# A gated-DeltaNet stage on one core: inverses of 16x16 blocks on GpSimd, and a regrouped chunk

## The chip, the cores and the metric

The kernel runs on one core of a Trainium2 chip. The metric is device time of one execution in microseconds (us). Three runs of the kernel before gave 1876.74 us (median), 1874.43 and 1877.13. Everything is float32.

## The reference

Two layers over 512 latent tokens and 256 context tokens, 1024 channels. Each layer has an input projection, latent attention (4 heads), a bidirectional gated DeltaNet (4 heads of 128), a pooling branch, an output projection and a mixture of experts. The change is in the DeltaNet alone. The reference computes it in chunks, for every chunk and head:

```python
decay = exp(where(incl, gc[:, None] - gc[None, :], -inf))
a_low = where(strict, (kb @ k.T) * decay, 0.0)       # kb = k * beta
tmat  = a_low + eye(C)
w = solve(tmat, kb * exp(gc)); u = solve(tmat, v * beta)   # unit lower triangular
qk = (q @ k.T) * decay
# then, chunk after chunk, with the state s
v_new = u - w @ s
o     = (q * exp(gc)) @ s + qk @ v_new
s     = s * exp(g_last) + (k * exp(g_last - gc)).T @ v_new
```

The backward direction runs the same on reversed tokens, over context and then latent tokens too.

## The kernel before

The 768 tokens are six tiles (chunks) of 128 tokens, j = 0 to 5; in chunk j both directions d = 0, 1 work, each on its own tile, with four heads h. Everything of the stage is kept transposed: state `minus_S`, keys, queries, decays `gE` and `gQG`.

For every chunk the kernel builds X, the inverse of the unit triangular 128x128 matrix, by doubling. Each half of 64 rows is treated apart, for both directions and four heads at a time. The identity minus the entries inside blocks of 2 is the inverse at level 0. At level n = 1 to 5 (blocks of 2, 4, 8, 16, 32) GpSimd (POOL) cuts the entries that join two blocks out of the matrix (`masked`, semaphore `ml`), TensorE (PE) multiplies them by the transposed inverse (`level_factor`, L955), VectorE (DVE) writes identity minus that into `gW` (L2391), PE multiplies once more for both X and its transpose (`level_update`, L973), and ScalarE (ACT) copies the four products back to `gXC` (L1887). Each step of a level waits for the one before. A last step joins the two halves: `z6` (L1058), ACT's two negated copies (L1892), `u6` (L1070), DVE's copies into `gX`. POOL copies the diagonal halves into `gX` (L2830, semaphore `xd`), and `v` of the chunk, the product X by the right side, needs all of it.

The rest of the chunk's work is put between the levels, by a table `BETWEEN`: 13 slots per chunk, slot 2n-1 between the two products of level n and slot 2n behind them. Its entries are `v` (L889), `go` (output, L900 and L901), `st` (state update, L906), `kr` (keys turned, L871), `kk` (key-key products of the next chunk, L863), `ks` (values turned, minus keys by state, L879 and L882), `qk` (query-key products of the next chunk, L866) and `g` (decays of the next chunk). In layer 0 one half of a modulation load (`ada_load`, L571, eight matmuls and 1 MB of weights per pair of halves) stands in each of slots 0 to 11. Each engine walks the same slots in its own program order. Banks of PSUM go round in a ring of eight.

Ahead of the stage stands the attention, 24 calls (tile, head) in layer 0 and 16 in layer 1; the first chunk's `g`, `kk` and level 0 are set among its last eight calls (`first_chunk`). ACT's exponentials of call n are L1855. POOL does next to nothing there.

In the first chunk ACT also has eight SiLU passes (L1727, L1874) and two loads of its function table.

## Time and profile before

| | us |
|---|---|
| median of three runs | 1876.74 |
| lowest and highest | 1874.43, 1877.13 |
| profiled execution, whole | 1878.56 |
| its span, first to last instruction | 1876.4 |
| PE busy | 1765.4 (94%) |
| DVE, ACT, POOL busy | 716.7, 471.4, 433.8 |

The profile is of one execution. Busy time of PE counts modelled ends of pipelined matmuls. A matmul of float32 stands in the profile as two instructions, so 16 matmuls of the program are x32. The recurrent stage, the subject here, lies from 365.9 to about 590 us (layer 0) and from 1337.9 to about 1520 us (layer 1). A chunk is counted from the end of one `u6` (L1070) to the end of the next.

### The profile page before, as it was taken

Reading aid. Unit: us, or ns where it says so; the run is one execution under the profiler, and the core shown is the slowest. Engines: PE = TensorE matmul, PEld = TensorE weight load, DVE = VectorE, ACT = ScalarE, POOL = GpSimd, SP = SyncE. Lnnn points to the kernel's source line nnn. Section 1 sums busy time; section 2 is a strip of 40 time slices with the busy share of each in tenths; the row PEclk is TensorE's granted clock in tenths of the full one; section 3 lists DMA queues with packets and bytes.
Section 4 is the critical chain, followed back from the end, with each engine's and each line's share of the span. In section 5 each row is a group of like instructions: output and inputs, shape, how many; then the busy total and the mean of one; then the engine's idle time right before and its main releaser. Section 6 shows DMA issues by size and latency. Waiting matters only on the chain.

```text
span 1876.4 us, 40908 instructions
## 1 busy us (share of the span) xinstructions
PE 1765.4 (94%) x17273; PEld 1087.7 (58%) x17273; DVE 716.7 (38%) x1452; ACT 471.4 (25%) x1051; POOL 433.8 (23%) x556
## 2 busy tenths in 40 slices
PE   6999999989999998999999999999888899899998
PEld 4565556667776554655566455556577854445544
DVE  3045233455554234111211506334466633432323
ACT  4211422443234041111110321333433222101010
POOL 2713000255651003111110142200277710000000
PEclk9999999999999998999999999999999999999999
DMA  9510000265555217999998421000300022599996
GB/s 311 169 60 23 23 0 1 96 202 188 181 174 206 67 45 272 344 372 371 366 328 326 122 67 45 23 1 2 103 26 14 15 113 90 222 408 413 408 413 240
DMA packets 140855, 321.24 MB, mean 171 GB/s; under 512 B 11208, under 2 KB 98894, under 8 KB 125358
## 3 DMA queue, kind: packets, MB, share of 16 engines
q1 hardware_dynamic: 127584, 287.20, 41.2%
q0 software_dynamic: 6432, 20.00, 4.1%
q10 hardware_dynamic: 6702, 12.05, 2.0%
q8 instruction: 107, 1.75, 0.4%
q14 instruction: 30, 0.25, 0.0%
HBM read 305.77 MB, written 13.45 MB: 170 GB/s over the span
## 4 chain that ended last, share of the span: by engine, by line
PE 84%; DVE 7%; issue 3%; ACT 2%; DMA 2%; SPq 1%; POOL 0%; ACTq 0%; DVEq 0%; POOLq 0%
PE psum L654 16%; PE psum L1204 12%; PE psum L1104 7%; PE psum L1235 6%; PE psum L786 3%; PE psum L1213 3%; PE psum L1285 3%; PE psum L973 3%; PE psum L807 2%; PE psum L571 2%; PE psum L955 2%; PE psum L679 2%; PE psum L1247 2%; PE psum L889 1%; PE psum L839 1%
## 5 line engine op out<-in xcount | busy, mean ns | idle before, releaser
L654 PE MATMUL psum<-hT,ring 128*128 128x512 f32 (+3 forms) x880 | 298.9, 497 | 0.0
L654 PEld LDWEIGHTS psum<-hT,ring 128*128 128x128 f32 (+1 forms) x880 | 165.7, 190 | 121.3 <-issue 111.0
L1204 PE MATMUL psum<-ring,arena 128*64 128x256 f32 x1536 | 176.3, 387 | 6.0 <-DVE xT L2553 3.6
L1204 PEld LDWEIGHTS psum<-ring,arena 128*64 128x64 f32 x1536 | 110.1, 139 | 69.4 <-issue 14.9
L1104 PE MATMUL psum<-hT,ring 128*128 128x512 f32 (+1 forms) x384 | 139.4, 521 | 0.9 <-DVE xT L2437 0.9
L2524 DVE TENSOR_TENSOR arena<-arena,psum 128x384 f32<-128x384 f32 (+1 forms) x32 | 15.6, 488 | 260.8 <-PE psum L1213 159.8
L1104 PEld LDWEIGHTS psum<-hT,ring 128*128 128x128 f32 x384 | 72.7, 190 | 64.8 <-issue 61.5
L973 PE MATMUL psum<-wbuf,ring 64*64 64x64 f32 x1920 | 76.1, 225 | 30.6 <-DVE wbuf L2391 18.9
L1887 ACT COPY ring<-psum 128x256 f32<-128x256 f32 x240 | 72.8, 382 | 127.6 <-PE psum L973 127.6
L2870 POOL DMA_INDIRECT big<-h_rows_lat,idx x16 | 15.7, 979 | 377.9 <-PE psum L1309 175.4
L2391 DVE TENSOR_TENSOR wbuf<-lev,psum 128x256 f32<-128x256 f32 x120 | 45.1, 417 | 137.0 <-PE psum L955 137.0
L973 PEld LDWEIGHTS psum<-wbuf,ring 64*64 64x64 f32 x1920 | 66.6, 137 | 49.2 <-issue 47.7
L2553 DVE SCALAR_TENSOR_TENSOR xT<-psum,modraw,xT 128x512 f32<-128x512 f32 (+1 forms) x136 | 79.7, 621 | 18.8 <-PE psum L1285 12.8
L786 PE MATMUL psum<-hT,ring 128*128 128x256 f32 (+1 forms) x192 | 80.8, 530 | 0.0
L1965 ACT COPY arena<-psum 128x512 f32<-128x512 f32 (+2 forms) x49 | 23.6, 481 | 221.2 <-PE psum L1226 147.1
L2176 DVE SCALAR_TENSOR_TENSOR big<-psum,cols,big 128x511 f32<-128x511 f32 (+1 forms) x44 | 27.6, 628 | 126.9 <-ACT big L1720 125.9
L973 PE MATMUL psum<-ring,wbuf 64*64 64x64 f32 x1920 | 73.5, 225 | 1.2 <-issue 1.2
L1285 PE MATMUL psum<-arena 128*128 128x512 f32 x144 | 65.8, 602 | 4.4 <-DVE arena L2540 2.7
L1969 ACT ACTIVATE arena<-psum 128x384 f32<-128x384 f32 (+1 forms) x32 | 14.0, 438 | 212.5 <-PE psum L1204 107.6
L973 PEld LDWEIGHTS psum<-ring,wbuf 64*64 64x64 f32 x1920 | 63.0, 137 | 1.6 <-issue 1.5
L571 PE MATMUL psum<-ring,scol 128*32 128x256 f32 x768 | 60.2, 399 | 3.5 <-issue 2.6
L2223 DVE TENSOR_REDUCE small<-psum 128x1 f32<-128x768 f32 (+1 forms) x40 | 33.9, 851 | 77.2 <-PE psum L807 75.3
(358 smaller groups left out, 3327.8 us busy)
## 6 DMA issues: line engine op xcount, KB each, us to landing
ring<-in_moe_w_gate SPq DMA_DIRECT2D x64, 1024.0 KB, 10.5
ring<-in_ada_w SPq DMA_DIRECT2D x48, 1024.0 KB, 5.4
ring<-in_moe_w_up SPq DMA_DIRECT2D x32, 1024.0 KB, 9.7
hT<-in_moe_w_down SPq DMA_DIRECT2D x24, 1024.0 KB
ring<-in_w_in SPq DMA_DIRECT2D x20, 1024.0 KB, 7.3
big<-in_moe_w_up SPq DMA_DIRECT2D x16, 1024.0 KB, 10.8
sz<-in_moe_w_down SPq DMA_DIRECT2D x16, 1024.0 KB
big<-in_moe_w_down SPq DMA_DIRECT2D x16, 1024.0 KB
```

Source lines behind the costliest of these rows:

```text
L571: m = pe.matmul(ada[1][r:r + 32, 0:SLOT_COLS], lhsT=scol[:, 2 * k:2 * k + 32], rhs=ada[2][:, k, :], start=half == 0, stop=half == 1)
L654: m = pe.matmul(b[0:c1 - c0, 0:n], lhsT=w[:, k, c0:c1], rhs=hT[:, k, t0:t0 + n], start=k == 0, stop=k == KD - 1)
L786: x = pe.matmul(b[:, 0:n], lhsT=w[:, k, m % 2 * P:(m % 2 + 1) * P], rhs=hT[:, k, t0:t0 + n], start=k == 0, stop=k == KD - 1)
L973: m = pe.matmul(bs[kind][o, i * HALF:(i + 1) * HALF], lhsT=v if transposed else w, rhs=w if transposed else v, start=True, stop=True)
L1104: m = pe.matmul(b[:, 0:x], lhsT=w[:, k, c:c + P], rhs=mixT[:, k, t0:t0 + x], start=k == OUT_REST[0], stop=k == OUT_GDN[-1])
L1204: m = pe.matmul(b[e * CAP_L:(e + 1) * CAP_L, 0:2 * P], lhsT=xs[:, k, e, 0:CAP_L], rhs=w[e][:, 2 * (k - ks[0]) + q, :], start=k == 0, stop= ...
L1213: m = pe.matmul(b[r:r + CAP_C, 2 * P:3 * P], lhsT=xs[:, k, e, CAP_L:CAP], rhs=v[:, 2 * (k % (KD // 2)) + q, f * P:(f + 1) * P], start=k == ...
L1235: m = pe.matmul(ys[c][e * CAP_L:(e + 1) * CAP_L, :], lhsT=hidT[:, q, f * P + e * CAP_L:f * P + (e + 1) * CAP_L], rhs=w[e][:, f, c * 512:(c ...
L1285: m = pe.matmul(b[:, 0:SEQ], lhsT=ylat[:, k * P:(k + 1) * P], rhs=Sl[:, :], start=True, stop=True)
L1887: read_out(act.copy(gXC[j % 2][:, d, w:w + GH, :].rearrange("p h c -> p (h c)"), b), key)
L2391: read_out(dve.tensor_tensor(gW[:, :, h0:h0 + 2, :], eyes, b, ALU.subtract), key)
L2553: read_out(dve.scalar_tensor_tensor(out=x, in0=b[:, 0:n], scalar=mods_of[l][:, 5 * KD + k, 1 - g:2 - g], in1=x, op0=ALU.mult, op1=ALU.add) ...
```

## The change

Levels 1 to 3 are gone. The inverses of all 16x16 diagonal blocks, of both directions, six tiles and four heads, are made once per layer during the attention: 3072 bytes per partition, one block per 256 numbers, three blocks in each of the 128 partitions ("lanes").

- In attention call 1 PE makes the key-key products of 32 tokens each (`pk`, 96 matmuls of 128x32 by 32 columns, four beside each other in the output partitions); DVE keeps the 16x16 diagonal blocks. In call 2 ACT writes them to device memory (`kkD`, pieces of 64 bytes), POOL reads them back as lanes, together with decay sums and beta.
- POOL takes differences, ACT the two functions of them (call 7), POOL multiplies, and then solves by 15 steps of an outer product and a subtraction, each waiting for the one before. POOL writes the inverses out (`xD`), ACT reads them back per chunk (`blocks_back`), POOL spreads them over the block diagonal (`spread`), and PE turns them (`diagonal_blocks`) as it did with level 0.
- ACT waits in the third last attention call for the inverses to be written.
- A chunk now has levels 4 and 5 and 7 slots. `qk` of a chunk stands at that chunk's end instead of the end of the one before, `kk` and the turned blocks of the next chunk beside it, both `ks` in one slot, both `v` in one slot. In layer 0 both halves of a modulation load stand in each of slots 0 to 5.
- The decays of the next chunk are no longer subtracted on DVE: ACT takes the four heads with a bias each. They stand in slots 3 and 5.
- On POOL the one-sided decays and the masks follow the copies of the diagonal halves.

```diff
 BETWEEN = (
-    (("v", 0),), (("v", 1),), (("go", 0),), (("go", 1),), (("st", 0), ("st", 1)),
-    (("g", 0),), (("g", 1), ("kr", 0)), (("kr", 1),), (("kk", 0),), (("kk", 1),), (("ks", 0),), (("qk", 0),),
-    (("ks", 1), ("qk", 1)))
-G_SLOTS = (6, 8)
+    (("v", 0), ("v", 1)), (("go", 0),), (("go", 1),), (("st", 0), ("st", 1)),
+    (("kr", 0), ("kr", 1), ("kk", 0)), (("ks", 0), ("ks", 1)), (("kk", 1), ("t0", 0), ("qk", 0), ("qk", 1)))
+G_SLOTS = (3, 5)
+LANES_EXP = 7
...
+                    if n == 1:
+                        pe.wait_ge(s["lmul"], GH)
+                        for w in range(2):
+                            b = claim(("pk", l, w))
+                            for x in range(NT * GH // 2):
+                                i, h = divmod(w * NT * GH // 2 + x, GH)
+                                for q in range(4):
+                                    t = slice(i * P + 32 * q, i * P + 32 * (q + 1))
+                                    m = pe.matmul(b[32 * q:32 * (q + 1), 32 * x:32 * (x + 1)], lhsT=qkvT[:, GH + h, t],
+                                                  rhs=qkvT[:, GH + h, t], start=True, stop=True)
...
-                    for n in range(1, LEVELS - 1):
-                        pe.wait_ge(s["ml"], (LEVELS - 1) * j + n + 1)
+                    for n in range(FROM, LEVELS - 1):
+                        pe.wait_ge(s["ml"], 2 * j + n - FROM + 1)
                         level_factor(j, n, x)
-                        gdn_between(j, 2 * n - 1)
-                        if n == 1:
-                            pe.wait_ge(s["x0"], j + 1)
+                        gdn_between(j, 2 * (n - FROM) + 1)
                         for d in range(2):
                             level_update(j, n, x, d)
-                        gdn_between(j, 2 * n)
+                        gdn_between(j, 2 * (n - FROM) + 2)
...
+                def next_decays(j, d):
...
+                    for h in range(GH):
+                        m = act.activation(e[:, h, :], q[:, h, :], ACT.Abs, bias=gc[:, d, i, h:h + 1], scale=-1.0)
+                    m.then_inc(s["away"], 1)
...
+                    act.activation(e, e, ACT.Exp, scale=-1.0).then_inc(s["away"], 1)
+                    act.activation(q, q, ACT.Exp).then_inc(s["away"], 1)
...
+                    act.copy(gt4[:, j % 2, d, 0, :], e[:, :, end])
+                    act.copy(gt4[:, j % 2, d, 1, :], q[:, :, end]).then_inc(s["dex"], 1)
...
+                    if slot in G_SLOTS and 1 <= j < NT - 1:
+                        next_decays(j + 1, G_SLOTS.index(slot))
+                    if slot == 4 and j + 2 < NT:
+                        act.wait_ge(s["x0"], j + 2)
+                        blocks_back(j + 2)
...
+                    if n == 2:
+                        for w in range(2):
+                            evacuated(act, ("pk", l, w))
+                        act.dma_start(kkD[l].rearrange("x p c -> p x c"), pairs16).then_inc(s["pairs"], 16)
...
+                    if n == 5:
+                        act.wait_ge(s["xout"], 32 * (l + 1))
+                        blocks_back(0)
+                        blocks_back(1)
...
+                pool.tensor_tensor(lane_y, across(lane_g), down_(lane_g), ALU.subtract).then_inc(s["ldiff"], 1)
+                pool.wait_ge(s["lexp"], 2 * (l + 1))
+                link(pool.tensor_tensor(lane_a, lane_a, lane_y, ALU.mult), l)
...
+                for k in range(BLOCK - 1):
+                    n, w = BLOCK - 1 - k, k + 1
+                    t = lane_t[:, 0:3 * n * w].rearrange("p (s r c) -> p s r c", s=3, r=n)
+                    link(pool.tensor_tensor(t, lane_a[:, :, w:BLOCK, k:w].to_broadcast([P, 3, n, w]),
+                                            lane_y[:, :, k:w, 0:w].to_broadcast([P, 3, n, w]), ALU.mult), l)
+                    x = lane_y[:, :, w:BLOCK, 0:w]
+                    link(pool.tensor_tensor(x, x, t, ALU.subtract), l)
...
+                    if j >= 2:
+                        decay_state(j - 1, 0)
+                    if j + 1 < NT:
+                        spread(j + 1)
+                    if j >= 2:
+                        decay_state(j - 1, 1)
                     if j:
+                        decayed_keys(j, 0)
+                        decayed_keys(j, 1)
                         queries(j)
                     if j + 1 < NT:
                         decays(j + 1)
...
                     pool.wait_ge(s["xd"], j + 1)
                     if j + 1 < NT:
-                        begin(j + 1)
+                        one_sided(j + 1)
+                        masks(j + 1)
```

Two places show how instructions moved. The first is PE in layer 1, from the end of a full chunk into the next one. Before: L879 and L882 are `ks` of direction 1, L866 `qk`, L933 the turned blocks, L889 `v`, L955 and L973 the two products of level 1.

```order
L879 MATMUL psum<-ident,big 128x128
L882 MATMUL psum<-arena 128x128
L866 MATMUL psum<-big 128x128 x4
L933 MATMUL psum<-lev,mlaw 64x64 x16
L889 MATMUL psum<-arena,ring 128x128 x4
L955 MATMUL psum<-ring,mlaw 64x64 x16
L889 MATMUL psum<-arena,ring 128x128 x4
L973 MATMUL psum<-wbuf,ring 64x64 x2
```

Now: L1104 is `u6`, L885 `kk`, L958 the turned blocks, L888 `qk`, L911 `v`, L980 the first product of level 4, L922 and L923 `go`.

```order
L1104 MATMUL psum<-wbuf,ring 64x64 x8
L885 MATMUL psum<-big 128x128 x4
L958 MATMUL psum<-lev,ring 64x64 x16
L888 MATMUL psum<-big 128x128 x8
L911 MATMUL psum<-arena,ring 128x128 x8
L980 MATMUL psum<-ring,mlaw 64x64 x16
L922 MATMUL psum<-arena 128x128
L923 MATMUL psum<-arena 128x128
```

`ks` has moved ahead of `u6`; `kk`, the turned blocks and both `qk` stand between `u6` and `v`; and from the first factor PE goes to `go` and level 4.

The second place is ACT in layer 1, within a full chunk. Before: L1887 are the copies of X, L1795 to L1802 the decays of the next chunk (directions 0 and 1), L1892 the copies of `z6`.

```order
L1887 COPY ring<-psum 128x256 x8
L1795 ACTIVATE arena<-arena 128x512
L1797 ACTIVATE small<-small 128x8
L1800 ACTIVATE arena<-arena 128x512
L1802 ACTIVATE arena<-arena 128x512
L1887 COPY ring<-psum 128x256 x4
L1795 ACTIVATE arena<-arena 128x512
L1797 ACTIVATE small<-small 128x8
L1800 ACTIVATE arena<-arena 128x512
L1802 ACTIVATE arena<-arena 128x512
L1887 COPY ring<-psum 128x256 x4
L1892 ACTIVATE wbuf<-psum 128x128 x2
```

Now: L1964 are the copies of X, L1841 to L1849 the decays of direction 0 and, last row, the first of direction 1, L1854 the blocks of the chunk after next, L1969 the copies of `z6`.

```order
L1964 COPY ring<-psum 128x256 x4
L1865 DMA arena<-decay_rows 128x512
L1841 ACTIVATE arena<-arena,small 128x128 x4
L1845 ACTIVATE arena<-arena 128x512
L1846 ACTIVATE arena<-arena 128x512
L1848 COPY small<-arena 128x4
L1849 COPY small<-arena 128x4
L1964 COPY ring<-psum 128x256 x4
L1854 DMA blocks_in<-inverse_blocks 128x4x16 x2
L1969 ACTIVATE wbuf<-psum 128x128 x2
L1841 ACTIVATE arena<-arena,small 128x128 x4
```

The decays of direction 0 stand ahead of the last level's copies, those of direction 1 behind the copies of `z6`.

## Rows read from the trace of the kernel before

**Rows 1.** windows: length, busy us and (xcount) by engine, granted clock, DMA share, GB/s

```profile
365.90:590.00 224.10, 203.74 (x4522) 155.38 (x4523) 116.00 (x245) 81.41 (x224) 122.45 (x147) 0.98 0.61 194
1337.90:1520.00 182.10, 152.47 (x3861) 135.16 (x3860) 108.56 (x235) 65.49 (x187) 114.82 (x141) 0.96 0.08 25
472.30:510.40 38.10, 34.56 (x769) 26.71 (x770) 21.48 (x44) 12.39 (x36) 23.24 (x28) 1.00 0.57 183
1421.30:1452.50 31.20, 26.96 (x675) 24.28 (x674) 20.87 (x45) 9.76 (x30) 22.91 (x27) 1.00 0.07 20
365.90:399.50 33.60, 27.48 (x661) 18.87 (x661) 15.58 (x35) 20.21 (x46) 14.89 (x20) 0.95 0.74 237
1337.90:1364.00 26.10, 17.30 (x537) 14.78 (x538) 13.34 (x32) 17.39 (x40) 9.48 (x15) 0.86 0.23 74
```

**Rows 2.** timeline of PE, layer 0: start us, us, engine, line, out<-in, count

```profile
403.22 0.69 PE L955 MATMUL psum<-ring,mlaw 64*64 64x64 f32 x32
403.85 1.16 PE L889 MATMUL psum<-arena,ring 128*128 128x128 f32 x8
...
405.51 0.27 PE L973 MATMUL psum<-wbuf,ring 64*64 64x64 f32 x2
...
406.60 0.60 PE L901 MATMUL psum<-arena 128*128 128x128 f32 x3
```

**Rows 3.** waits of PE in the recurrent stage of layer 1

```profile
PE psum L973 <- DVE wbuf L2391: 16.1, 17, 1.5
```

**Rows 4.** timeline of PE, a full chunk of layer 1

```profile
1428.14 0.49 PE L900 MATMUL psum<-arena 128*128 128x128 f32 x2
...
1430.12 0.69 PE L955 MATMUL psum<-ring,mlaw 64*64 64x64 f32 x32
```

**Rows 5.** timeline of ACT, the same chunk

```profile
1441.16 0.63 ACT L1795 ACTIVATE arena<-arena 128x512 f32<-128x512 f32 x1 [1.75 <-DVE small L2268]
...
1442.84 1.17 ACT L1887 COPY ring<-psum 128x256 f32<-128x256 f32 x4
...
1450.42 0.45 ACT L1892 ACTIVATE wbuf<-psum 128x128 f32<-128x128 f32 x2 [2.02 <-PE psum L1058]
```

**Rows 6.** timeline of POOL, the same chunk

```profile
1445.75 1.04 POOL L2710 TENSOR_TENSOR arena<-arena,small 128x512 f32<-128x512 f32 x1 [1.70 <-ACT arena L1802]
1446.75 2.50 POOL L2721 TENSOR_TENSOR arena<-arena,tri 128x512 f32<-128x512 f32 x2
1449.40 0.39 POOL L2830 COPY ring<-ring 64x256 f32<-64x256 f32 x1 [0.16 <-POOL arena L2721]
...
1451.24 0.72 POOL L2731 TENSOR_TENSOR mlaw<-dT,lev 128x256 f32<-128x256 f32 x1
```

**Rows 7.** timeline of DVE, the same chunk

```profile
1437.20 1.28 DVE L2318 TENSOR_TENSOR arena<-arena,psum 128x512 f32<-128x512 f32 x2
```

**Rows 8.** DMA issues: KB each, median us to landing

```profile
arena<-decay_rows ACTq DMA_DIRECT2D x20, 256.0 KB, 4.0
```

**Rows 9.** timeline of ACT, first chunk of layer 1

```profile
1337.86 1.28 ACT L1727 ACT_TABLE_LOAD   x1
1339.16 0.85 ACT L1727 ACTIVATE big<-big 128x768 f32<-128x768 f32 x1
```

**Rows 10.** timeline of PE in the attention, products into 64 output partitions

```profile
1307.04 0.27 PE L839 MATMUL psum<-wbuf,arena 128*64 128x128 f32 x1
...
1307.15 0.27 PE L839 MATMUL psum<-wbuf,arena 128*64 128x128 f32 x1
```

**Rows 11.** timeline of ACT in the attention of layer 1

```profile
1284.86 0.91 ACT L1855 ACTIVATE ring<-psum,small 128x768 f32<-128x768 f32 x1
...
1317.11 0.91 ACT L1855 ACTIVATE ring<-psum,small 128x768 f32<-128x768 f32 x1
```

**Rows 12.** timeline of POOL in the attention of layer 1

```profile
1303.45 1.04 POOL L2710 TENSOR_TENSOR ring<-ring,small 128x512 f32<-128x512 f32 x1 [108.67 <-ACT ring L1802]
```

**Rows 13.** DMA queues (packets, MB, share of 16 engines)

```profile
q10 hardware_dynamic: 6702, 12.05, 2.0%
```

More of the change, by code:

```diff
@@ L49 @@
 LEVELS = 7
+BLOCK = 16
+FROM = 4
 HALF = P // 2
@@ L305, in build_program @@
         gc = small[:, 96:144].rearrange("p (d i h) -> p d i h", d=2, i=NT)
+        beta = small[:, 144:192].rearrange("p (d i h) -> p d i h", d=2, i=NT)
+        gc_beta = small[:, 96:192]
+        lane_g = small[:, 192:240].rearrange("p (s r) -> p s r", s=3)
+        lane_b = small[:, 240:288].rearrange("p (s r) -> p s r", s=3)
         krp = small[:, 436:628].rearrange("p (i c) -> p i c", i=NT)
@@ L948, in level_factor @@
                         for i, pair in enumerate(((0, 3), (1, 2))):
-                            if i and n > 1:
+                            if i and n > FROM:
                                 evacuated(pe, ("x", l, j, d, n - 1))
@@ L1804, in decay_rows, with blocks_back @@
+                def blocks_back(j):
+                    for d in range(2):
+                        act.dma_start(blocks_in[:, j % 2, d * GH:(d + 1) * GH, :],
+                                      xD[l][d, tile_of(d, j)].rearrange("h p c -> p h c")).then_inc(s["xin"], 16)
                 def decay_rows(j, d):
@@ L1880, in _ @@
                     gdn_between(j, 0)
-                    for n in range(1, LEVELS - 1):
-                        gdn_between(j, 2 * n - 1)
+                    for n in range(FROM, LEVELS - 1):
+                        gdn_between(j, 2 * (n - FROM) + 1)
                         for d in range(2):
@@ L2384, in _ @@
                 for j in range(NT):
-                    if j:
-                        inverse_of_blocks(j)
-                    for n in range(1, LEVELS - 1):
+                    for n in range(FROM, LEVELS - 1):
+                        gdn_between(j, 2 * (n - FROM))
                         for h0, name in ((0, "zo"), (2, "zd")):
@@ L2693, in _ @@
                     m.then_inc(s["row2"], 1)
-                pool.wait_ge(s["gbd"], 1)
-                pool.wait_ge(s["lmul"], GH)
-                product_ready(pool, ("gc", l))
+                pool.wait_ge(s["pairs"], 16 * (l + 1))
+                for d in range(2):
+                    pool.dma_start(lane_a[d * HALF:(d + 1) * HALF].rearrange("p s r c -> p (s r c)"),
+                                   kkD[l].rearrange("x p c -> (x p c)").rearrange("(m e) -> m e", e=LANE)
+                                   ).then_inc(s["lanes"], 16)
@@ new lines, in _, with across, down_ @@
+                pool.wait_ge(s["grow"], 16)
+                pool.dma_start(small[:, 192:288].rearrange("p (w x) -> p w x", w=2),
+                               gD[l].rearrange("w d i h c -> w (d i h c)").rearrange("w (m x) -> m w x", x=3 * BLOCK)
+                               ).then_inc(s["lanes"], 16)
+                pool.wait_ge(s["lanes"], 48 * (l + 1))
+                def across(rows_, n=P):
+                    return rows_.unsqueeze(3).to_broadcast([n, 3, BLOCK, BLOCK])
+                def down_(rows_, n=P):
+                    return rows_.unsqueeze(2).to_broadcast([n, 3, BLOCK, BLOCK])
@@ L2727, in masked @@
                     a = gA if j else gA0
-                    first = a[:, :, 0:2, :] if n == 0 else a[:, :, GH:GH + 2, :]
-                    second = a[:, :, 2:8:5, :] if n == 0 or n % 2 else a[:, :, 2:4, :]
-                    mask = lev[:, :, n, :].unsqueeze(2).to_broadcast([P, 2, 2, HALF])
+                    first = a[:, :, GH:GH + 2, :]
+                    second = a[:, :, 2:8:5, :] if n % 2 else a[:, :, 2:4, :]
+                    mask = lev[:, :, n - FROM, :].unsqueeze(2).to_broadcast([P, 2, 2, HALF])
@@ L2791, in _ @@
                 decays(0)
-                begin(0)
-                third_mask(0)
+                masks(0)
+                how = freed_by[lent_prior[l]]
+                product_ready(pool, how[0], how[1])
+                spread(0)
                 pool.wait_ge(s["att"], 1)
                 one_sided(0)
-                pool.wait_ge(s["ml"], 3)
+                pool.wait_ge(s["ml"], 2)
                 if l == 0:
```

309 lines of the change are left out of this document (166 added, 143 removed).

## The prediction

> **What bounds the kernel now.** I read the windows first. The recurrent stage is 224.1 us in layer 0 and 182.1 us in layer 1, 406.2 of a span of 1876.4, and PE is busy for 203.74 and 152.47 of it; the reader is to see that no other engine reaches 70% there [rows 1]. A full chunk of layer 0 takes 38.1 us with 34.56 of PE, one of layer 1 31.2 with 26.96 [rows 1]. So layer 0 is bound by how much PE has to do, and layer 1, without modulation loads, by PE and some waiting. The table of waits says for what: in layer 1 second products of a level (L973) wait 17 times, 16.1 us in all, for DVE's copy between the two products [rows 3]. Then the timelines of one chunk give the price of a step on each engine [rows 2, 4 to 7]. The attention ahead keeps PE nearly full, while POOL stands idle for 108.67 us in layer 1 before its first decay [rows 12]: that is where the new work goes.
>
> **What goes.** A level packed without a wait is one factor, 403.22 to 403.85, 0.63 us, and two updates, 405.51 to 406.60, 1.09 us: 1.72 us of PE [rows 2]. Three of five go in each of six chunks and two layers: 36 x 1.72 = 62 us of PE, 31 per layer. With them go 36 x 4 copies on ACT and as many handoffs, whose waits are the rest of the gain or its loss, depending on what stands in their place. Four of the six masks of a chunk go from POOL, and the subtraction of decays from DVE; neither bounds anything.
>
> **The chunk that is left, layer 1.** PE's own work is 26.96 - 3 x 1.72 = 21.8 us [rows 1, 2]. Against it stands a loop through the other engines, since the decays have moved next to the copies. From the first state product of a chunk: `st` on PE 1.1 (eight instructions as L889, 403.85 [rows 2]), its addition on DVE 0.64 [rows 7], ACT's decays of direction 0, the last copies of X 1.2, `z6` 0.4 (half the instructions of a factor), its two copies 0.45, the decays of direction 1, POOL's beta product 1.04, four copies of 0.45 (0.39 and the handoff) 1.8, two one-sided decays 2.5, the first mask, two instructions of 0.72, 1.4, the factor 0.63, `go` 1.98, the update 1.09, `go` 1.98, the factor 0.63 [rows 2, 4 to 7]. ACT's decays of one direction are four passes over 128, two over 512 and two tiny ones. A pass over 128 is 0.22 (two in 0.45), one over 512 0.63, at a pitch of some 0.53 [rows 5]: 0.9 + 1.1 + 0.2 and two handoffs of 0.15, 2.5. The sum is 21.8 with the decays twice; 15 handoffs of 0.15 (0.16 is what POOL's wait for itself shows [rows 6]) make it 24.1. So the loop, not PE, sets a full chunk of layer 1: 24 us for 31.2, a gain of 7. With neither handoffs nor queues behind each other it would be 22, with 0.3 a handoff and the two issues of `blocks_back` in line 27. I take 24, because the masks and decays stand back to back on POOL already. `go` and its `qk` are missing in chunks 1 and 2 of this layer, so their loop is some 4 us shorter, and PE idles about 4.6 us in each.
>
> **Layer 0.** PE's own work of a full chunk is 34.56 - 5.2 = 29.4 [rows 1]. The loop is 24 plus two slots of loads inside it, which cost PE half of 34.56 - 26.96 = 7.6 at most: under 28. So PE bounds it still, and I add 1 us for what does not fit: 30.4 for 38.1. The loads have the same bytes in less time: 183 GB/s become 230, and the first chunk moves 237 already [rows 1], so the queue hides them.
>
> **First chunk.** Here ACT becomes the bound. It has the table load 1.3, eight SiLU passes of 0.85 and less [rows 9], a second table load, and, new, both directions' decays of chunk 1 ahead of the last copies, 5 us. In layer 1 that is 1.3 + 5.5 + 1.3 + 5 + 8 copies of 0.3 = 15.5 from 1337.86, so `z6` comes at about 1353.5 and `u6` ends near 1355: 17 us instead of 26.1. Layer 0 adds the loads' copies and issues, about 7: 24.5 instead of 33.6. PE is idle for some 9 us in each.
>
> **Sum of the stage.** By PE's busy time: layer 0 203.7 - 31 = 172.7, idle 9 in the first chunk, 1 in each other and 1.5 in the tail, 188, so 36 less. Layer 1: 152.5 - 31 = 121.5, idle 9, twice 4.6, twice 2.3, and 2 at the end, 146, so 36 less. By chunks instead (9 + 7 + 3 x 7.7 + 3.5, less 2.2 for the `qk` that moved behind the last `u6`) layer 0 gives 40, layer 1 about 42. The two counts differ by tails of matmuls that the busy time holds and a chain does not. I take 74 for both layers, nearer to the busy count, which has fewer of my own steps in it.
>
> **What the attention gets.** (a) PE: 96 products are 192 instructions per layer. Into 64 output partitions and 128 columns one takes 54 ns (two in 0.107 us at L839 [rows 10]), into quarters of 64x64 20 ns (32 in 0.63 [rows 2]). So 3.8 to 10.4 us; the new ones have 32 columns and four stand beside each other, nearer to the second: 5. (b) DVE and ACT in the same calls: two masks from PSUM, two additions, the decay sums two calls after the gates instead of many; PE waits 1.5 for the chain gate, sum, copy. Together 6.5 per layer, 13, with 8 and 26 as ends. (c) The lanes on POOL. An instruction of n elements costs 0.19 + 0.0021 n us (128x256 0.72, 128x512 1.25 [rows 6]) and 0.16 for its wait. Fifteen steps handle 3 x 680 elements twice, 4080: 8.5 + 30 x 0.35 = 19. Three products of 768 are 5.8, clearing and turning 2.8: 27.6 us. In layer 1 ACT makes the two functions in call 7, at 1284.86, 1.8 us long, and wants the inverses in call 13, at 1317.11 [rows 11]: 32.3 - 1.8 = 30.5 us, less a landing of 4.0 or under [rows 8]. That is a draw; what ACT waits there holds up the copies and exponentials of the last three calls. Ends: 0, and with POOL twice as slow 27. I take 2. In layer 0 there are 14 calls between, so nothing. (d) The pieces of 64 bytes, 3072 of them to write: a packet of ACT's queue takes 0.02 x 16 x 1876 / 6702 = 90 ns on one of 16 engines [rows 13], at 1.8 KB each, so 17 us at most and likely under half. It fits between calls 2 and 7.
>
> A rule that speaks against (c): POOL's instructions here cost 2.1 ns an element [rows 6]. The Trainium skill, GPSIMD Engine Reference, section 7, says that a read whose step is over 8 bytes costs half as much again for each element. No row here has such a step. If all of the solver's products paid it, they would take 4 us longer by that page, which makes the wait in layer 1 likelier and changes no term of mine.
>
> (e) The clock. In the stage's first chunk, where PE waits most, the granted clock reads 0.86 in layer 1 and 0.95 in layer 0, and 1.00 in full chunks [rows 1]. That is 26.1 x 0.14 = 3.7 us lost; PE will be idle there for 9 us at a stretch, so I add 3 for both layers, with 0 and 10 as ends.
>
> **Total.** -74 + 13 + 2 + 3 = -56. The profiled execution took 1878.56, 1.8 above the median of the runs, so 1822.5 of its kind and 1821 for the median.
>
> **Rivals.** *More is hidden* (6%): handoffs cost 0.05 and the chain count of the stage holds, -82 + 8: 1803. For it speaks that PE's gaps in full chunks are small now; against it the loop. *The lanes come late in layer 1* (15%): rows too short for POOL's pace, a solver of 45 us instead of 27.6; ACT stands in call 13 for 17 us with three calls' exponentials and copies behind it, POOL's masks and DVE's `kk` behind those: 1838. *The loop bounds both layers* (13%): 28 us in layer 1 and 33.5 in layer 0, as ACT's queue of loads' issues, decays, `blocks_back` and copies is one line: 7 x 4 more, 1850. For it speaks that PE's wait in L973 is already 16.1 us [rows 3]. *Slower* (5%): the same solver, at 70 us or above. The slack is 30 us in layer 1 and, 14 calls for 6, about 70 in layer 0; so layer 1 loses T - 28 and layer 0 T - 70, which eats the 56 at T = 77, 2.8 times my sum; 1881 at 80. Against it: 680 elements a lane is little, and even a fixed 1 us for each of 30 instructions makes only 45 in all. *It does not do what it says* (1%): the levels are gone from PE's order, so hardly.
>
> **Chances.** My forecast 60%, its own range 1808 to 1834. Faster 0.93, within 0.2% (what a measurement here can tell, 3.8 us) 0.02, slower 0.05. The range goes from 1802, past the terms' favourable ends, to 1854, past the loop rival.
>
> **What would show it.** Chunks of 30 and 24 us; first chunks of 24.5 and 17 with an idle stretch of PE under ACT's decays; 36 x 48 products fewer; the solver's 30 instructions in under 30 us, ending before the third last call of layer 1; attention 6 to 9 us longer. I am wrong if full chunks of layer 1 stay above 27, if ACT stands waiting for the written inverses, or if POOL has instructions of over 1 us for under 200 elements.

## The result, and the profile after

The changed kernel took 1801.4 us (median of 4 runs, 1800.3 to 1807.1) beside 1876.9 for the kernel before on the same chip: a ratio of 0.960, 95% interval 0.958 to 0.963. The forecast was 1821 with a range of 1802 to 1854. It is faster by 75 us, not by 56, and the time lies 0.6 us below the lower end of that range (the same kernel run again, 1805.5, lies inside it).

The profiled execution spans 1798.7 us. Its windows (length, busy time and instruction count of PE, PEld, DVE, ACT and POOL, granted clock, DMA share, GB/s) stand in the order of [rows 1]: the stage of each layer, a full chunk of each, the first chunk of each.

```profile
380.70:556.00 175.30, 162.89 (x2800) 130.05 (x2799) 85.95 (x183) 69.24 (x193) 89.36 (x106) 0.95 0.80 251
1308.10:1446.00 137.90, 115.62 (x2134) 105.80 (x2134) 79.10 (x171) 54.22 (x156) 81.50 (x100) 0.94 0.13 34
464.15:491.70 27.55, 26.76 (x481) 21.84 (x481) 14.75 (x32) 10.31 (x33) 17.71 (x21) 1.00 0.80 256
1391.80:1414.80 23.00, 20.77 (x385) 19.34 (x386) 14.58 (x34) 8.06 (x26) 17.31 (x21) 1.00 0.09 25
380.70:410.20 29.50, 20.41 (x347) 13.83 (x345) 7.36 (x17) 18.63 (x42) 10.68 (x14) 0.71 0.87 277
1308.10:1327.20 19.10, 11.17 (x250) 9.87 (x249) 6.89 (x15) 15.61 (x36) 5.67 (x10) 0.76 0.37 118
```

The reader is to see that a full chunk of layer 0 fell from 38.1 to 27.6 us with PE as full as ever, and one of layer 1 from 31.2 to 23.0 with 2.2 us of PE's time idle. The first chunks gained less, and their clock is 0.71 and 0.76, where it was 0.95 and 0.86.

To compare kernels I cut each layer in two: the attention, from its first exponential to the end of ACT's last copy, and the stage, from there to the end of the last update of the last chunk. All lengths below are cut so; us:

| kernel | attention L0 | L1 | stage L0 | L1 | median | ratio to before |
|---|---|---|---|---|---|---|
| before | 111.4 | 81.0 | 214.3 | 173.7 | 1876.9 | 1 |
| after | 127.9 | 86.2 | 164.0 | 127.7 | 1801.4 | 0.960 [0.958, 0.963] |
| after, run again | 127.7 | 87.8 | 164.0 | 128.2 | 1805.5 | 0.961 [0.957, 0.964] |
| levels out alone | 111.5 | 81.5 | 173.1 | 137.0 | 1800.1 | 0.957 [0.956, 0.959] |
| solver twice | 128.4 | 100.1 | 164.1 | 128.2 | 1819.3 | 0.968 [0.966, 0.970] |
| spread first | 125.9 | 83.7 | 163.4 | 128.6 | 1797.6 | 0.956 [0.955, 0.958] |
| masks first | 128.3 | 86.2 | 162.8 | 122.8 | 1800.3 | 0.958 [0.957, 0.960] |
| loads in separate groups | 128.9 | 86.1 | 169.0 | 128.2 | 1809.3 | 0.963 [0.961, 0.965] |
| `ks` in separate slots | 124.9 | 86.1 | 162.6 | 127.1 | 1803.5 | 0.960 [0.958, 0.962] |
| `pk` in separate calls | 124.9 | 86.0 | 164.9 | 128.5 | 1803.4 | 0.960 [0.957, 0.963] |
| `pk` twice | 132.8 | 93.4 | 165.3 | 128.3 | 1819.2 | 0.968 [0.966, 0.971] |
| combined | 121.1 | 84.5 | 162.8 | 122.6 | 1788.4 | 0.951 [0.948, 0.953] |

The same kernel moved by 4 us from one comparison to another, and layer 0's attention by 3 where nothing in it was changed (`ks` in separate slots). So differences of medians below 4 us are read from the stretches, not from the totals. Where that 3 comes from can be seen in the attention of layer 0 as a whole, first after, then `ks` in separate slots, then `pk` in separate calls:

```profile
252.77:380.68 127.91, 111.92 (x857) 73.94 (x857) 48.86 (x114) 34.93 (x86) 31.62 (x50) 0.96 0.07 17
252.65:377.58 124.93, 109.04 (x857) 72.01 (x857) 48.85 (x114) 34.96 (x86) 31.62 (x50) 0.99 0.07 18
254.36:379.27 124.91, 112.03 (x857) 74.06 (x857) 48.68 (x114) 34.96 (x86) 31.62 (x50) 0.96 0.08 18
```

The first two kernels give PE the same 857 instructions in the same order. It is busy 2.9 us longer at a granted clock of 0.96 than at 0.99, and the stretch is 3.0 us longer. So the clock moves this stretch by 3 us between executions of the same code. The third is as short at the lower clock.

The stage gave back 50.2 + 46.0 = 96.2 us and the attention took 16.6 + 5.2 = 21.7 (worked out before rounding). That leaves 74.5 of the 77.7 between the spans.

What binds a full chunk of layer 0 now, PE in the trace of after (start us, us, engine, line, out<-in, count):

```profile
464.08 1.16 PE L885 MATMUL psum<-big 128*128 128x128 f32 x8
465.17 0.69 PE L958 MATMUL psum<-lev,ring 64*64 64x64 f32 x32
465.79 2.05 PE L888 MATMUL psum<-big 128*128 128x128 f32 x16
467.68 1.95 PE L911 MATMUL psum<-arena,ring 128*128 128x128 f32 x16
...
500.82 1.07 PE L593 MATMUL psum<-ring,scol 128*32 128x256 f32 x16
```

There is no gap: keys with keys, turned blocks, queries with keys and `v` follow each other. The last row, from the next chunk, is a modulation load's product pair, 16 instructions in 1.07 (1.00 to the next group's start); before, 8 took 0.64 and came in twice the number of places.

What PE waits for in the stage of layer 1 (us in all, times, longest), the answer to [rows 3]:

```profile
PE psum L1092 <- ACT ring L1964: 8.4, 5, 4.5
PE psum L980 <- POOL mlaw L2846: 6.8, 5, 1.9
PE psum L998 <- DVE wbuf L2472: 3.8, 4, 1.0
```

DVE's copy between the two products, 16.1 us before, is down to 3.8. ACT's copies ahead of `z6` (L1092) and POOL's masks (L2846) have taken its place: the loop that the prediction wrote down.

### The profile page after: what moved, and what is told of

It reads as the page before. It is cut to its first block and busy times, and to the rows that moved or that the text cites. A ratio compares the mean times of both kernels' runs of the same rounds, so it can differ in the third digit from the quotient of the medians.

```text
span 1798.7 us, 34350 instructions
## 1 busy us (share of the span) xinstructions
PE 1691.2 (94%) x14201; PEld 1036.1 (58%) x14201; DVE 657.7 (37%) x1330; ACT 448.8 (25%) x991; POOL 414.8 (23%) x556
## 3 DMA queue, kind: packets, MB, share of 16 engines
q10 hardware_dynamic: 25646, 13.08, 2.7%
## 5 line engine op out<-in xcount | busy, mean ns | idle before, releaser
L2977 POOL DMA_INDIRECT big<-h_rows_lat,idx x16 | 15.7, 983 | 377.0 <-PE psum L1343 173.7
L2633 DVE SCALAR_TENSOR_TENSOR xT<-psum,modraw,xT 128x512 f32<-128x512 f32 (+1 forms) x136 | 79.7, 621 | 18.7 <-PE psum L1319 12.7
L2253 DVE SCALAR_TENSOR_TENSOR big<-psum,cols,big 128x511 f32<-128x511 f32 (+1 forms) x44 | 27.6, 628 | 127.4 <-ACT big L1754 126.5
L829 PE MATMUL psum<-arena 96*128 96x256 f32 (+1 forms) x144 | 53.5, 491 | 8.2 <-ACT arena L1931 5.1
L1238 PE MATMUL psum<-big,arena 128*64 128x256 f32 x256 | 59.6, 381 | 0.0
L553 PE MATMUL psum<-lev 128*128 128x512 f32 x128 | 58.6, 609 | 0.0
L1269 PE MATMUL psum<-hT,arena 128*64 128x512 f32 x192 | 58.4, 598 | 0.0
L1269 PE MATMUL psum<-sz,arena 128*64 128x512 f32 x128 | 58.4, 598 | 0.0
L593 PE MATMUL psum<-ring,scol 128*32 128x256 f32 x768 | 53.1, 400 | 2.6 <-DMA ring<-in_ada_w 2.6
L2760 POOL TENSOR_TENSOR arena<-arena,rown 128x384 f32<-128x384 f32 x22 | 21.9, 995 | 136.3 <-DVE arena L2243 136.3
```

Of the source, the lines that this page charges most:

```text
L553: pe.matmul(psum[:, b, :], lhsT=lev[:, 0, 0:2, :], rhs=lev[:, 0:2, 0:4, :], start=True, stop=True)
L593: m = pe.matmul(ada[1][r:r + 32, 0:SLOT_COLS], lhsT=scol[:, 2 * k:2 * k + 32], rhs=ada[2][:, k, :], start=half == 0, stop=half == 1)
L829: m = pe.matmul(b[:, k0 * P:(k0 + nk) * P], lhsT=QT[0:QK, h, i * P:(i + 1) * P], rhs=KT[0:QK, h, k0 * P:(k0 + nk) * P], start=True, stop=True)
L1238: m = pe.matmul(b[e * CAP_L:(e + 1) * CAP_L, 0:2 * P], lhsT=xs[:, k, e, 0:CAP_L], rhs=w[e][:, 2 * (k - ks[0]) + q, :], start=k == 0, stop= ...
L1269: m = pe.matmul(ys[c][e * CAP_L:(e + 1) * CAP_L, :], lhsT=hidT[:, q, f * P + e * CAP_L:f * P + (e + 1) * CAP_L], rhs=w[e][:, f, c * 512:(c ...
L2253: link(dve.scalar_tensor_tensor(out=a, in0=b[:, 0:n - 1], scalar=cols[:, COL_CONV + m: COL_CONV + m + 1], in1=a, op0=ALU.mult, op1=ALU.add ...
```

## The experiments

**The levels alone.** The kernel before, without levels 1 to 3: their masks, factors, copies and updates are left out and nothing stands in for them, so the inverses aren't the reference's.

```diff
                     for n in range(1, LEVELS - 1):
-                        pe.wait_ge(s["ml"], (LEVELS - 1) * j + n + 1)
-                        level_factor(j, n, x)
+                        if n >= 4:
+                            pe.wait_ge(s["ml"], 3 * j + 3)
+                            level_factor(j, n, x)
                         gdn_between(j, 2 * n - 1)
```

> The kernel before with levels 1 to 3 left out on every engine and nothing else changed: the 13 slots, their order, the decays on DVE and the attention are those of before. The three levels' part of the inverse is not computed. Theory (the stage shrank both by the levels and by the regrouping): PE loses 36 x 1.72 = 62 us, a full chunk of layer 0 goes from 38.1 to about 32 us and of layer 1 from 31.2 to about 26, total 1877 - 70 = about 1807. Rival (the levels alone are the whole gain of the stage, 96 us): chunks of 27 and 23 us as after the change, total about 1781.

Measured: stages of 173.1 and 137.0, 77.9 us less than before, which is 2.16 for each of 36 levels. The attention didn't change. A full chunk of layer 0 and the 27.1 us chunk of layer 1 in this kernel:

```profile
450.62:480.80 30.18, 28.62 (x481) 21.69 (x482) 18.64 (x38) 8.48 (x24) 18.96 (x22) 1.00 0.72 230
1361.50:1388.56 27.06, 23.74 (x385) 21.80 (x386) 19.24 (x39) 6.17 (x18) 18.91 (x22) 0.87 0.07 22
```

PE's busy time in layer 0 fell by 34.56 - 28.62 = 5.9, 1.98 a level; the rest of the 2.16 is waits and, in layer 1, the clock. The changed kernel has the same number of PE instructions in these chunks (481 and 385) and does them in 27.6 and 23.0. So what changed in the stage beside the levels (the order of the pieces, the decays on ACT, the order on POOL) is worth 18.3 us, 9.0 in layer 0 and 9.3 in layer 1. In layer 0 both chunks have the clock at 1.00. In layer 1 the chunk above has 0.87 and the next one, 27.0 us long, 0.94, where the changed kernel has 1.00. These two are equally long at different clocks, which speaks against the clock as the whole of the 9.3, but its part is not shown. And the total is that of the changed kernel: what the lanes cost in the attention, 21.7 us, the new order nearly pays for.

**The modulation loads in separate groups.** The changed kernel with one half of a load ahead of the slot's pieces and one behind.

```diff
                 def gdn_between(j, slot):
 
+                    if l == 0 and slot < ADA_CHUNK:
+                        ada_load(0)
                     for what, i, d in between(j, slot):
...
                         if slot < ADA_CHUNK:
-                            ada_load(0)
                             ada_load(1)
```

> The changed kernel with the two halves of a modulation load set apart again, one ahead of the slot's pieces and one behind them, as the kernel before had them in slots of their own. Theory (part of the stage's surplus in layer 0 is that groups of matmuls stand together: a pair of halves takes 1.00 us where two single ones took 1.14): 36 x 0.14 = 5 us more, layer 0's full chunks 28.0 to 28.4 for 27.2 to 27.9. Rival (it is only the levels and waits): chunks as they are, under 1 us.

Measured: stage of layer 0 169.0 for 164.0, layer 1 unchanged. A full chunk has the same instructions and PE is busy for 0.93 us more:

```profile
466.24:494.76 28.52, 27.69 (x482) 21.24 (x481) 14.93 (x32) 9.81 (x31) 17.10 (x20) 1.00 0.78 242
```

Over the five chunks behind the first, PE's busy time is 4.8 us longer. So 5.0 of layer 0's 9.0 us come from the two halves of a load standing behind each other. The total rose by some 4 to 8.

**Masks ahead of the one-sided decays.** POOL's order behind the copies of a chunk.

```diff
                     if j + 1 < NT:
-                        one_sided(j + 1)
                         masks(j + 1)
+                        one_sided(j + 1)
```

> The changed kernel with POOL's masks of the next chunk set ahead of its one-sided decays. Theory (in layer 1 a loop through ACT and POOL sets the chunk, and PE waits 6.8 us in all for the mask of level 4): full chunks of layer 1 go from 23.0 to about 21.8, layer 0 stays, total 4 to 6 us less. Rival (the qk products of the next chunk then wait on DVE for the one-sided decays and give it back): under 1.5 us less, or more time.

Measured: stage of layer 1 122.8 for 127.7, layer 0 162.8 for 164.0. PE's waits in the stage of layer 1, and its two full chunks:

```profile
PE psum L1092 <- ACT ring L1964: 8.7, 5, 4.9
PE psum L998 <- DVE wbuf L2472: 3.8, 4, 1.0
PE psum L980 <- POOL mlaw L2846: 2.4, 2, 1.3
1368.26:1392.10 23.84, 20.84 (x385) 19.33 (x385) 16.93 (x39) 8.07 (x26) 17.26 (x21) 1.00 0.12 28
1392.10:1413.73 21.63, 20.66 (x386) 19.31 (x385) 14.44 (x33) 8.06 (x26) 17.27 (x21) 1.00 0.09 27
```

The wait for the mask fell from 6.8 to 2.4, the two largest others stayed, and the stage got 5.0 shorter. So the loop through POOL set layer 1's pace, and layer 0, where PE is full, hides it. The chunks don't gain alike: 18.7, 23.8, 21.6 and 19.7 us for 21.4, 23.0, 23.0 and 21.1. The first of the two full ones still has a mask wait of 1.3 us and is 0.9 longer than before the swap; only the second is as short as expected. And the first of the four ran at a clock of 0.92 after and at 1.00 here, so some of its 2.7 may be the clock's.

**The solver twice.** POOL's 15 steps are issued twice over, the second time on their own result, so the inverses aren't the reference's.

```diff
-                for k in range(BLOCK - 1):
+                for k in list(range(BLOCK - 1)) * 2:
```

> The changed kernel with the 15 steps on POOL done twice over (30 more instructions, 15.9 us by the profile after). The second pass spoils the inverses. Theory (in layer 1 ACT's wait in call 13 has under 2 us to spare, in layer 0 over 40): layer 1 loses 14 to 16 us, layer 0 nothing, total 1801 + 15 = 1816. Rival (the wait has room, or other work fills it): no change, under 3 us.

The solver's first and last rows in the changed kernel, layer 1, on POOL:

```profile
1263.23 0.28 POOL L2807 TENSOR_TENSOR mlaw<-sz,mlaw 128x45 f32<-128x45 f32 x1
...
1270.56 0.55 POOL L2807 TENSOR_TENSOR mlaw<-sz,mlaw 128x192 f32<-128x192 f32 x1
...
1278.74 0.27 POOL L2810 TENSOR_TENSOR mlaw<-mlaw 128x45 f32<-128x45 f32 x1
1279.08 1.49 POOL L2811 COPY sz<-mlaw 64x768 f32<-64x768 f32 x1
```

Its 30 instructions take 1279.08 - 1263.23 = 15.85 us. Done twice, layer 1's attention grows to 100.1, by 13.9 against the first profile of the changed kernel and by 12.4 against the second (87.8), and layer 0's by 0.5. ACT in layer 1, solver twice:

```profile
1286.49 0.91 ACT L1931 ACTIVATE ring<-psum,small 128x768 f32<-128x768 f32 x1
...
1302.75 2.05 ACTq L1854 DMA_DIRECT2D blocks_in<-inverse_blocks  x4
1304.89 0.37 ACT L1942 COPY ring<-psum 128x256 f32<-128x256 f32 x1 [17.40 <-issue]
```

ACT stands for 17.4 us ahead of the reads of the inverses, with an attention copy behind them. In the changed kernel the exponential at 1284.21 is followed at 1284.56 by these reads. In both kernels they start 3.1 us behind the start of POOL's second write issue (1281.44, and 1299.66 with the solver twice), so the reads themselves have no slack: they begin as soon as the inverses are there. The slack is in what PE still has to do behind them. PE's wait for the sums of the softmax (L829, for DVE's L2317) grows from 1.2 to 11.4 us, by 10.2; the clock falls meanwhile, and the same two groups of products behind the wait take 2.93 and 1.87 us for 1.56 and 1.05. Waits and clock together leave a slack of 15.85 less 12.4 to 13.9, some 2 to 3.5 us; in layer 0 it is at least 15. "Late lanes" is a real mechanism that starts just where the kernel stands.

**The spread ahead of the masks, first chunk.** POOL spreads the inverses that PE turns at the attention's end before it makes masks.

```diff
                 decays(0)
-                masks(0)
                 how = freed_by[lent_prior[l]]
                 product_ready(pool, how[0], how[1])
                 spread(0)
+                masks(0)
```

> The changed kernel with POOL's spread of the first chunk's blocks set ahead of the first chunk's two masks. Theory (PE waits 2.9 and 2.4 us in the last attention call for POOL's spread, which stands behind masks that wait for DVE's kk): both waits go, total 4 to 5 us less. Rival (the blocks come back from memory as late as the masks are done, or DVE is late next): under 1.5 us less.

PE's longest waits in layer 0's attention, the kernel after:

```profile
PE psum L829 <- ACT arena L1931: 4.6, 3, 1.7
PE psum L1051 <- ACT arena L1931: 3.7, 3, 2.8
PE psum L1051 <- DVE arena L2317: 3.1, 1, 3.1
PE psum L958 <- POOL ring L2864: 2.9, 1, 2.9
```

The last of these, and its twin of 2.4 in layer 1, are gone with the spread first. The attention is 2.0 and 2.5 shorter, and the median 1797.6. The ratio's interval, 0.955 to 0.958, ends where that of the changed kernel begins, but overlaps that of its second run (0.957 to 0.964), so the gain is read from the two waits.

**`ks` in separate slots.** The last product of decayed keys with the state moved one slot later.

```diff
-    (("kr", 0), ("kr", 1), ("kk", 0)), (("ks", 0), ("ks", 1)), (("kk", 1), ("t0", 0), ("qk", 0), ("qk", 1)))
+    (("kr", 0), ("kr", 1), ("kk", 0)), (("ks", 0),), (("ks", 1), ("kk", 1), ("t0", 0), ("qk", 0), ("qk", 1)))
```

> The changed kernel with the keys-by-state product of direction 1 moved from ahead of u6 to behind it, so that the two products of keys with the state no longer stand together. Theory (the pair covers ACT's two copies of z6, 0.5 us and a handoff, and one product of 1.4 us covers that as well): no difference in either layer, under 1.5 us. Rival (standing together is what keeps PE from waiting before u6, or v is later by its DVE step): 0.5 to 1 us a chunk, 5 to 10 us more.

Measured: stages of 162.6 and 127.1 for 164.0 and 127.7, median 1803.5 for 1801.4 and 1805.5. That both `ks` stand together is worth nothing that can be told, in either direction.

**`pk` in separate calls.** Half of the 96 small products in call 1 and half in call 2.

```diff
-                    if n == 1:
+                    if n in (1, 2):
                         pe.wait_ge(s["lmul"], GH)
-                        for w in range(2):
+                        for w in (n - 1,):
```

> The changed kernel with the second half of the 32-token products moved from attention call 1 to call 2. Theory (after 179 short instructions PE stands for 2.1 us with nothing that it waits for; half as many at once do not run its queue dry): 2 to 4 us less over both layers in calls 1 to 3. Rival (the gap is a wait for the bank or for what follows, and comes with the second half wherever it stands): no difference, or the lanes' start and thereby layer 1's wait in call 13 comes later by 1 to 4 us.

PE in layer 0's attention, first after, then `pk` in separate calls:

```profile
256.90 1.74 PE L1013 MATMUL psum<-big 128*32 128x32 f32 x179
260.72 0.32 PE L1013 MATMUL psum<-big 128*32 128x32 f32 x13 [2.08 <-issue]
260.97 1.56 PE L808 MATMUL psum<-hT,ring 128*128 128x256 f32 x4
```

```profile
258.63 1.03 PE L1013 MATMUL psum<-big 128*32 128x32 f32 x96
259.59 1.56 PE L808 MATMUL psum<-hT,ring 128*128 128x256 f32 x4
...
261.73 1.34 PE L1013 MATMUL psum<-big 128*32 128x32 f32 x96
263.00 0.62 PE L1020 MATMUL psum<-small,tri 128*128 128x24 f32 x4
```

The standstill of 2.08 us behind the 179th record of a small product, which nothing on another engine releases, is not there. The attention of layer 0 is 3.0 shorter. That is as much as with `ks` in separate slots, but not for the same reason: there the clock was 0.99, here it is 0.96 as in the changed kernel, and PE's busy time is the same (112.03 for 111.92). The 2.9 us are gained by the fifth exponential, just behind the small products. Layer 1's attention, which has no standstill, is 0.1 shorter, and the median, 1803.4, can't show 3 us.

**`pk` twice.** Each small product issued a second time into the same place.

```diff
-                            for x in range(NT * GH // 2):
+                            for x in list(range(NT * GH // 2)) * 2:
```

> Every one of the 192 small products of keys in call 1 of each layer's attention is issued twice, the second into the same place. Theory A: the small products cost what their records show, 9.7 ns each, and the 2.1 us of standing behind them is bound to the group, not to its number: 192 more in each layer cost 1.9 us a layer, 3.7 us in all, 1805 for 1801.4, and the gap stays near 2.1 us. Theory B: the gap is the price of the number of small instructions in a row, as what feeds PE can't keep up with them: then it doubles too, 4 us a layer, 8 in all, 1809.5. Theory C: the attention hides it, since the exponentials of ACT set its pace: no change.

> The changed kernel as it is, once more, beside the run of doubled products: it tells how far the same kernel moves from one call of runs to another. 1801.4 was its median; within 3 us of it, if differences of 2 to 3 us between kernels of different calls mean nothing. In layer 0's attention (127.9 us in its first profile, with a granted clock of 0.86 in the last 20 us) 125 to 128.

Measured in one comparison: 1819.2 against 1805.5 for the kernel as it is, 13.8 us more, and more than any of the three theories gave. The attention is 5.1 and 5.6 longer than in the second profile of the changed kernel, the rest is spread. PE in layer 0, `pk` twice:

```profile
258.13 1.71 PE L1013 MATMUL psum<-big 128*32 128x32 f32 x179
262.05 1.31 PE L1013 MATMUL psum<-big 128*32 128x32 f32 x128 [2.21 <-issue]
265.78 1.28 PE L1013 MATMUL psum<-big 128*32 128x32 f32 x77 [2.42 <-issue]
266.99 2.93 PE L808 MATMUL psum<-hT,ring 128*128 128x256 f32 x4
```

A record of a small product shows 10 ns while the run lasts, but after 179 PE stands, and again after exactly 128. From 262.05 to 265.78 the 128 take 3.73 us, 29 ns each. The theory that the gap grows with the number of instructions is right in kind, and its price of 4 us a layer was low. Why the total grows by 3 us more than the two attentions isn't settled; 4 us is what the same kernel moves between comparisons, and the mean clock of the two profiles differs too (0.976 and 0.978).

**Combined.** Spread first, masks first, and in layer 0 the key products of the first chunk one call earlier; and ACT's two functions of the lanes, for which POOL waits 12.5 us in layer 1 of the changed kernel, one call earlier too.

```diff
-LANES_EXP = 7
+LANES_EXP = 6
...
-                    if n in (5, 6):
-                        gdn_piece("kk", 0, n - 5)
+                    if n in ((4, 5) if l == 0 else (5, 6)):
+                        gdn_piece("kk", 0, n - (4 if l == 0 else 5))
```

> The changed kernel with four changes together: the first spread ahead of the first masks, masks ahead of one-sided decays in every chunk, in layer 0 the first kk one attention call earlier (as before the change), and ACT's two functions of the lanes in call 6 for 7. Theory (the waits are at different places): 4.5 + 5 for the first two, 3 for the kk of layer 0, whose DVE work no longer falls into the call in which PE waits 3.1 us for it, and 0 to 1 for the last: 1801 - 12 = 1789. Rival (the kk of call 20 collides elsewhere and ACT waits for the lanes in call 6): 1794 or more.

Measured: 1788.4 (1784.8 to 1791.1, 5 runs), ratio 0.951 with an interval that lies below that of the changed kernel: it beats both. PE's waits in layer 0's attention:

```profile
PE psum L829 <- ACT arena L1931: 4.7, 4, 1.7
PE psum L1051 <- ACT arena L1931: 3.7, 3, 2.8
PE psum L1013 <- issue: 1.4, 1, 1.4
```

The waits of 3.1 for DVE and of 2.9 for POOL are gone, and the attention is 6.8 shorter; layer 1's stage keeps the 5 us of the masks. ACT's reads of the inverses in layer 1 now start 7.5 us behind the second write issue (1278.72 and 1271.23) where they started 3.1 behind it: that is slack.

## Why the prediction was right, and where its sizes were off

**Direction and mechanism held.** The levels' removal is most of the gain (77.9 of the stage's 96.2), PE bounds full chunks of layer 0, a loop through ACT and POOL those of layer 1. ("No other engine reaches 70%" misses the column of weight loads, 135.16 of 182.1 us in layer 1 [rows 1]; they are PE's own and changed nothing.) That loop was summed to 24.1 us and came to 23.0, and `masks first` shows that it is a bound: with a wait for the mask gone the stage is shorter. Two sizes were off, with opposite signs: stage -96.2 instead of -74, attention +21.7 instead of +15 (13 and 2). That the second error takes back 7 of the 22 of the first is luck.

**A level: 1.72 was too little.** I took the packed pitch of one factor and two updates [rows 2], which leaves out what stands around them. Without the levels PE's busy time fell by 1.98 each and the stage by 2.16: 77.9, where 36 x 1.72 gave 62. Of the 16 us between them, PE's own busy time is 36 x 0.26 = 9, if layer 1 goes by layer 0's full chunk. The other 7 are the waits, "the rest of the gain or its loss": a gain.

**The chunk that is left: nothing for the new order.** PE's own work was put at 29.4 and 21.8 and measured 26.8 and 20.8. The second reason beside the level is that I took every remaining piece at its old price. Side by side they cost less: `v` of both directions 1.88 for 2 x 1.09, a pair of load products 1.00 for 2 x 0.57 (`loads in separate groups`: 5.0 us for the stage). I then added 1 us a chunk "for what does not fit", and PE has 0.8 idle. Of two counts I took the one by busy time, 36 a layer, for having fewer of my own steps; the one by chunks, 40 and 42, was nearer to 50 and 46.

**First chunks.** Forecast 24.5 and 17, measured 29.5 and 19.1. ACT is the bound there, as said, and the first product behind its queue, `z6`, starts 24.2 us into layer 0's chunk, 1.7 later than 15.5 + 7. What I left out comes behind it. PE in the first chunk of layer 0, after:

```profile
387.60 1.07 PE L593 MATMUL psum<-ring,scol 128*32 128x256 f32 x16 [2.55 <-DMA ring<-in_ada_w]
390.18 1.22 PE L980 MATMUL psum<-ring,mlaw 64*64 64x64 f32 x32 [1.51 <-ACT ring L1964]
391.33 1.93 PE L593 MATMUL psum<-ring,scol 128*32 128x256 f32 x16
...
399.75 1.07 PE L593 MATMUL psum<-ring,scol 128*32 128x256 f32 x16
404.86 0.70 PE L1092 MATMUL psum<-ring 64*64 64x64 f32 x16 [4.03 <-ACT ring L1964]
405.49 1.97 PE L901 MATMUL psum<-ident,big 128*128 128x128 f32 x8
407.39 1.94 PE L593 MATMUL psum<-ring,scol 128*32 128x256 f32 x16
409.25 0.96 PE L1104 MATMUL psum<-wbuf,ring 64*64 64x64 f32 x16
```

The same load products take 1.07 us ahead of the wait of 4.03 and 1.94 behind it: the granted clock has gone from the 2.4 to the 1.2 GHz level. `ks`, a load pair and the last update fill 5.3 us from the start of `z6` to the end of the chunk, for which I had 2. Over the chunk the clock reads 0.71, in layer 1's 0.76. An earlier wait of the chunk was not in the forecast at all: 2.6 us for the weights of a load, though "the queue hides them". It and one of 1.5 us for ACT's copies stand around the first fall of the clock: the same load products take 1.07 us between them and 1.93 behind them. By the windows that is 29.5 x 0.29 + 19.1 x 0.24 = 13 us below full clock, where before had 33.6 x 0.05 + 3.7 = 5.4 [rows 1]. My 3 us for the clock was too little for that difference of 8, part of which lies beside ACT's queue and costs nothing; how much is not shown.

**Attention.** I had 6.5 for layer 0 and 8.5 for layer 1, with the wait for the lanes, and "6 to 9" as a sign. It was 16.6 and 5.2 (6.8 in the second profile). (a) The small products, 5 a layer: their rows sum to 2.1 us in layer 0 and 1.9 in layer 1, half of my lower end of 3.8. In layer 0 the standstill makes it 4.1 (256.90 to 260.97), near the 5 for a reason that I didn't have. (b) DVE and ACT: 1.5 a layer in the forecast. Layer 0 is where my step failed: I counted instructions for calls 1 to 3 and none for the last calls, where key products of the first chunk meet the softmax's sums on DVE (3.1 us, once) and the turned blocks wait for POOL (2.9). `combined` takes both out and gets 6.8 back. With 4.1 and 1.7 for the gate chain (a wait of 1.1 and its product) that is 11.8. For the other 4.8, PE's busy time in the attention grew by 5.8 with only 2.1 of `pk` in it. The clock accounts for about 3 of it: at 0.99 for 0.96 the same attention is 3.0 shorter (`ks` in separate slots). The last 2 are open. (c) The lanes: the solver was put at 19 us for 30 instructions and took 15.85. At 2.1 ns an element, fixed cost and wait together are (15.85 - 8.5) / 30 = 0.24, not 0.35. "A draw" was right: 2 to 3.5 us of slack. (d) Queue q10 went from 6702 to 25646 packets and its share of the 16 engines from 2.0 to 2.7%. That is about 177 us of one engine for 18944 packets, some 9 ns each where I had 90, and the pieces were there in time: POOL had taken its differences (L2795) and stood 12.5 us for ACT's functions before it went on.

The rule weighed against (c) is not tested by these runs. The products (L2807) read a column whose numbers lie 64 bytes apart, but each number is repeated over a whole row first, and the other operand is read along rows: from one element to the next the step is 0 or 4 bytes. They go from 0.28 to 0.55 us between 45 and 192 elements, 1.8 ns each; the subtractions (L2810), 0.30 and 0.58, cost the same. The Trainium skill, GPSIMD Engine Reference, section 7, has half as much again for a read with a step over 8 bytes and advises a small inner step; no run here shows it. The 4 us I gave it were also too much: half of 2.1 ns on the products' 2040 elements is 2.1, an estimate by that page.

**Rivals.** *More is hidden*, 1803, has the time, but not the reasons: its attention was +8 and its stage -82. *The loop bounds both layers* is excluded by 27.6 and 23.0 us, though its mechanism is what binds layer 1. *Lanes late* and *slower* need a solver that is longer than it was, and `solver twice` shows that layer 1 then pays: 12.4 to 13.9 us for 15.85.

## What to carry to other kernels

Price a piece that goes by the stretch in which it stood, waits and group starts included, and not by its packed pitch alone; and price the pieces that stay anew when they come to stand beside others of their shape. Work put under a busy engine is free only where the helper engines' queues have room at that moment: look at the last calls, where something waits for each of them, as well as at the ones that get the work. For a solver on POOL, the slack up to the first reader is the number to watch, since beyond it most of each microsecond is paid (12.4 to 13.9 of 15.85).

## What the runs showed of the hardware that was not expected

Very small matmuls (128x32 by 32 columns, four beside each other) show a record every 10 ns, but only for a stretch. PE then stands for 1.4 to 2.4 us with no engine named as the releaser: once in 192 records in layer 0, always behind the 179th, not at all in the 192 of layer 1, and twice in 384 in either layer. In the long run of them 128 took 3.73 us in layer 0, 29 ns each. Each matmul record has a weight load beside it, so 128 of them are 256 instructions. The Trainium skill, Runtime: NRT & Kernel Launch, section "Instruction fetch mechanics", says that instructions are fetched in blocks of 256 and that this is mostly hidden. The period of the standstills agrees with the block; that it is hidden doesn't hold for instructions this short.

The trace of `pk` twice has more: in each standstill a packet of 16384 bytes lands on the DMA queue q8, of the kind "instruction". In layer 0 these packets start at 259.35 and 263.09 us and take 1.14 and 1.35; PE stands from 259.84 and 263.36 and goes on at 262.05 and 265.78. In layer 1 they start at 1235.08 and 1238.61 and take 0.96 and 0.88; PE goes on at 1237.51 and 1240.97. So PE goes on 1.3 to 1.6 us after each packet has landed, four times of four. That makes fetching the likely cause. It is still argued from times that fall together: no run here isolates it.

The granted clock averages 0.71 over the first chunk of layer 0, where PE is busy for 20.4 of 29.5 us and waits 2.6, 1.5, 1.0 and 4.0 us, while the full chunks beside it have 1.00. What stands behind such a wait takes up to 1.8 times as long (1.94 for 1.07). So a wait of PE has a second price behind it: between 403.08 and 409.91 us, after the wait of 4.0, the clock is 0.50 and PE busy for 5.05 us, which at full clock would be about half, an estimate from the load products' 1.94 for 1.07.
